# MLA attention: value products once per head and the causal mask accumulated by TensorE

## The reference, cut to what matters

```
s = (einsum('bqhd,bkhd->bhqk', qn_b, k_nope) + einsum('bqhd,bkd->bhqk', qr_b, k_rope)) * scale
s = where(kpos[None, :] <= qpos[:, None], s, -inf)
p = softmax(s, axis=-1)
o = einsum('bhqk,bkhd->bqhd', p, v)
```

## Time and profile before

| | |
|---|---|
| time, median of three runs | 3065.33 us (3062.18 to 3070.17) |
| the profiled execution's own time | 3056.96 us |
| its span in the trace | 3055.2 us |
| TensorE busy | 2800.9 us, 92% of the span |
| VectorE busy | 1583.5 us, 52% |
| ScalarE busy | 873.3 us, 29% |
| the attention block, from its first product to the end of its last copy | 2527.8 to 2611.1 us |

### The profile page before, as it was taken

One profiled execution on the slowest core, in us unless ns is written; L12 is line 12 of the kernel. 1 busy time (PEld: TensorE's weight loads), 2 busy tenths in 40 slices (PEclk: granted clock), 3 DMA queues, 4 the chain that ended last, 5 costly groups with the idle time before them and its releaser, 6 DMA issues. The chain is left out here.

```text
span 3055.2 us, 40875 instructions
## 1 busy us (share of the span) xinstructions
PE 2800.9 (92%) x17603; PEld 2207.4 (72%) x17603; DVE 1583.5 (52%) x2140; ACT 873.3 (29%) x1121; POOL 369.5 (12%) x352
## 2 busy tenths in 40 slices
PE   8999999687879899999999999799999669999997
PEld 6888876577755777788887854578887545688886
DVE  5555455666686834555545326463454545463342
ACT  3222234111134232322213423332222334432221
POOL 1111010212010001111100001121121000120110
PEclk9999999899989999999999988899999879999999
DMA  5555531000030033455553210223343200222331
GB/s 148 166 169 162 162 114 39 13 3 3 21 101 14 28 93 98 115 161 158 165 172 114 84 42 0 69 71 107 107 143 104 55 31 29 69 83 97 97 97 55
DMA packets 267301, 272.02 MB, mean 89 GB/s; under 512 B 12607, under 2 KB 248103, under 8 KB 266928
## 3 DMA queue, kind: packets, MB, share of 16 engines
q1 hardware_dynamic: 251760, 207.53, 22.2%
q0 software_dynamic: 15360, 61.87, 6.2%
HBM read 267.28 MB, written 2.10 MB: 88 GB/s over the span
## 5 line engine op out<-in xcount | busy, mean ns | idle before, releaser
L915 DVE TENSOR_TENSOR mix_wl<-ring_raw,mix_wh 128x2048 fp32r<-128x2048 f32 (+2 forms) x66 | 153.1, 2320 | 221.5 <-ACT mix_wh L807 221.5
L707 PE MATMUL mix_ps<-h_mix_hi,mix_wh 128*128 128x512 f32 x624 | 244.4, 392 | 0.0
L709 PE MATMUL mix_ps<-h_mix_lo,mix_wh 128*128 128x512 f32 x624 | 242.8, 389 | 0.0
L807 ACT ACTIVATE mix_wh<-ring_raw 128x2048 fp32r<-128x2048 f32 (+2 forms) x66 | 117.6, 1782 | 210.9 <-PE mix_ps L713 162.1
L707 PE MATMUL ffn_ps<-h_rw_hi,ffn_wh 128*128 128x512 f32 x448 | 175.3, 391 | 0.0
L709 PE MATMUL ffn_ps<-h_rw_lo,ffn_wh 128*128 128x512 f32 x448 | 174.3, 389 | 0.0
L915 DVE TENSOR_TENSOR mlp_wl<-ring_raw,mlp_wh 128x2048 fp32r<-128x2048 f32 (+1 forms) x38 | 96.7, 2545 | 131.1 <-ACT mlp_wh L807 131.1
L915 DVE TENSOR_TENSOR mlp_wl<-mlp_raw,mlp_wh 128x2048 fp32r<-128x2048 f32 x36 | 93.2, 2589 | 134.4 <-ACT mlp_wh L807 134.4
L713 PE MATMUL mix_ps<-h_mix_hi,mix_wl 128*128 128x512 f32 x624 | 154.2, 389 | 0.0
L707 PE MATMUL mlp_ps<-view,mlp_wh 128*128 128x512 f32 x384 | 150.1, 391 | 0.0
L709 PE MATMUL mlp_ps<-view,mlp_wh 128*128 128x512 f32 x384 | 149.5, 389 | 0.0
(11 more groups left out here) (577 smaller groups left out, 6202.1 us busy)
## 6 DMA issues: line engine op xcount, KB each, us to landing
ring_raw<-in_mlp_w SPq DMA_DIRECT2D x32, 1024.0 KB, 5.4
mlp_raw<-in_mlp_w SPq DMA_DIRECT2D x32, 1024.0 KB, 5.3
ffn_sraw<-in_ada_w POOLq DMA_DIRECT2D x34, 768.0 KB, 5.2
ffn_raw<-in_ffn_w_gu SPq DMA_DIRECT2D x44, 512.0 KB, 5.1
ring_raw<-in_ffn_w_gu SPq DMA_DIRECT2D x44, 512.0 KB, 5.0
mix_sraw<-in_ada_w POOLq DMA_DIRECT2D x22, 768.0 KB, 5.2
ring_raw<-in_w_in SPq DMA_DIRECT2D x14, 1024.0 KB, 5.4
ring_raw<-in_a_w_in SPq DMA_DIRECT2D x12, 1024.0 KB, 5.3
```

The source lines that it names most:

```text
L707: nc.tensor.matmul(ps[:, it.banks[t], :], w(h, k, t), xh[:, k, :], start=it.first and k == it.k0, stop=False)
L709: nc.tensor.matmul(ps[:, it.banks[t], :], w(h, k, t), xl[:, k, :], start=False, stop=False)
L807: nc.scalar.activation(slot(wh, it), slot(raw, it), ACT.Copy).then_inc(hi_ready, 1)
L915: nc.vector.tensor_tensor(slot(wl, it), slot(raw, it), slot(wh, it).bitcast(F32), ALU.subtract)\
```

## The change

In `mla_attention`:

- The mask is no longer added by VectorE. `scores` gets a third product, the identity matrix times the mask, 128 columns, added onto the diagonal block of the score tile by TensorE. It is this product that signals that the scores are ready.
- TensorE, and no longer VectorE, waits for the mask to be loaded, ahead of its first product.
- `values` is called once per head, in the step in which it was called for the head's last unit before. It multiplies the values of key block j with all the probabilities of the queries from j*128 on: four products of 512, 384, 256 and 128 columns in place of ten of 128.
- `pT` holds a whole head (four blocks of 512 columns), with two buffers (h % 2). `copies` writes its block row into it with a stride; it waits for the values of head h - 2 at a head's first unit, and not for those of three units ago at each unit.

```diff
-        p, pT = sb("p", [P, 3, L]), sb("pT", [P, 3, L])
+        p, pT = sb("p", [P, 3, L]), sb("pT", [P, 2, TT, L])
...
-                nc.tensor.matmul(pS[:, n % 3, 0:w], qr[0:ROPE, h, ts], kr[0:ROPE, 0:w], start=False, stop=True)\
+                nc.tensor.matmul(pS[:, n % 3, 0:w], qr[0:ROPE, h, ts], kr[0:ROPE, 0:w], start=False, stop=False)
+                nc.tensor.matmul(pS[:, n % 3, i * P:w], e.ident[:, :], mask[:, :], start=False, stop=True)\
                     .then_inc(s_done, 1)
...
-            def values(n):
-                h, i = units[n]
-                pe.wait_ge(pT_ready, n + 1)
-                if i == 0 and h >= 2:
+            def values(h):
+                pe.wait_ge(pT_ready, TT * (h + 1))
+                if h >= 2:
                     pe.wait_ge(out_done, h - 1)
-                for j in range(i + 1):
-                    last = nc.tensor.matmul(po[:, h % 2, i * P:(i + 1) * P], v[:, j, h * P:(h + 1) * P],
-                                            pT[:, n % 3, j * P:(j + 1) * P], start=j == 0, stop=j == i)
+                for j in range(TT):
+                    last = nc.tensor.matmul(po[:, h % 2, j * P:L], v[:, j, h * P:(h + 1) * P],
+                                            pT[:, h % 2, j, j * P:L], start=j == 0, stop=j == TT - 1)
                 last.then_inc(used, 1)
 
+            pe.wait_ge(loaded, 16)
             for n in range(N + 3):
...
-                if n >= 3:
-                    values(n - 3)
+                if n >= 3 and units[n - 3][1] == TT - 1:
+                    values(units[n - 3][0])
...
-                diag = pS[:, b, i * P:(i + 1) * P]
-                then(nc.vector.tensor_tensor(diag, diag, mask[:, :], ALU.add))
                 then(nc.vector.reduce_max(mx[:, b:b + 1], pS[:, b, 0:(i + 1) * P], AX.X))
...
-            dve.wait_ge(loaded, 16)
...
-                if n >= 3:
-                    act.wait_ge(used, n - 2)
-                nc.scalar.activation(pT[:, n % 3, 0:(i + 1) * P], pt[:, n % 3, 0:(i + 1) * P], ACT.Copy)\
+                if h >= 2 and i == 0:
+                    act.wait_ge(used, h - 1)
+                nc.scalar.activation(pT[:, h % 2, 0:i + 1, i * P:(i + 1) * P],
+                                     pt[:, n % 3, 0:(i + 1) * P].rearrange("p (j t) -> p j t", t=P), ACT.Copy)\
                     .then_inc(pT_ready, 1)
...
-                    act.wait_ge(used, n + 1)
+                    act.wait_ge(used, h + 1)
```

## The result

The changed kernel takes 3076.18 us (median of 7 runs, 3075.0 to 3081.76) against 3066.24 for the kernel before (7 runs, 3060.94 to 3070.26). The ratio is 1.0039, with a 95% interval of 1.0027 to 1.005: 10 us slower where 6.0 were predicted. The median lies 4.9 us above the 3071.3 of the forecast, inside the range of 3063 to 3079, but beyond the 0.3% within which the likeliest case lay.

What follows compares the result with a forecast made beforehand. The block was taken to be bound by what TensorE must issue, plus 0.60 + 0.2 us of waiting per head. Seven terms summed to +6.0 us, giving 3071.3 us on the median, range 3063 to 3079.

Steps and rivals of the forecast that it cites:

- mask products: 32 mask products added to TensorE's stream, 0.22 us each: +7.0 us, bounds +3.2 and +10.2.
- value products: Per head, 20 value instructions of 128 columns become 8 of 512 to 128: -0.7 us, bounds -1.2 and +1.0.
- wait for the copy, and the slow restart: TensorE's wait for ScalarE's copy and the slower values behind it go, 0.28 us in seven heads: -2.0 us.
- wait for VectorE: TensorE's 0.60 us wait per head shrinks to 0.27 without VectorE's mask add: -2.3 us, bounds 0 and -4.2.
- wait for the mask at the start: TensorE's first product in the block now waits for the mask's load: +1.8 us, bounds 1.5 and 2.3.
- clock at the start: The 2.7 us pause before TensorE's first product may lower its clock: +0.9 us, bounds 0 and 1.7.
- tail: After the last scores, values wait for the head's last copy, mostly at low clock: +1.3 us, bounds -0.4 and +2.1.
- rival (a): Between rope pair and turn, the mask pair costs 0.32 us: sum +9.2, or +10.0 with the high tail; chance 0.18.
- rival (b2): Loads of short value products are on the path; 96 fewer save 3.1 us, not 0.7: sum +3.6 us; chance 0.05.
- rival (c): The chain through VectorE bounds the block; each unit gains 0.33 us: sum -7.5 us; chance 0.04.
- Rival (b): The mask on TensorE is nearly free, 0.10 us a pair: sum +2.2 us; chance 0.07.
- (d): Long value products stream no faster per column: 1.7 us more, 3073.0 us; counted within the forecast's chance of 0.66.

Runs made afterwards that it cites:

- e13: The changed kernel profiled once more, unchanged; not timed, block 96.2 us against 93.2 in its first execution, cycle 10.46 us.
- e4: The changed kernel with four 256-column products, result unused, on TensorE during its wait for the mask; ratio 1.0013 to the kernel before, block 89.9 us.
- e5: The changed kernel with the mask product between the nope and rope products; ratio 1.0045 to the kernel before, cycle 10.17 us.
- e11: Like e9, but with the mask accumulated by TensorE as in the change; ratio 0.9997 to the kernel before, cycle 10.02 us.
- e3: The changed kernel with the mask loaded once in the program's first block and kept in SBUF; ratio 1.0020 to the kernel before, block 89.2 us.
- e1: The changed kernel with the mask added by VectorE again, so only the values once per head; ratio 1.0017 to the kernel before, cycle 9.90 us.
- e8: The kernel before, with VectorE normalising a head's third unit before the fourth unit's maximum; ratio 1.0005 to the kernel before, cycle 9.98 us.
- e9: e1 with VectorE's order of e8 and the last head's values per unit; ratio 0.9980 to the kernel before, block 76.8 us.
- e12: The kernel of e1 profiled once more, unchanged; not timed, cycle 9.90 us, block 89.4 us.
- e7: The changed kernel with the mask kept from the first block and multiplied in the one-pass float32 form; ratio 1.0020 to the kernel before, cycle 10.03 us.

## Why the prediction was right or wrong

The direction and the place held, and four of the seven terms within 0.2 us, a fifth within 0.4. Two did not, and together they are nearly the whole miss in the profiled executions. By the sign set down beforehand (wrong above a cycle of 10.4 us) the measured 10.46 says so too: the price of the mask pair was wrong. Term by term, in us over the whole block:

| step | predicted | measured in the changed kernel |
|---|---|---|
| mask products | +7.0 | 8 x 1.12 = +9.0 |
| value products | -0.7 | 8 x (2.15 - 2.24) = -0.7 |
| wait for the copy, and the slow restart | -2.0 | gone, -2.0 |
| wait for VectorE | -2.3 | 7 x -0.27 = -1.9 |
| wait for the mask at the start | +1.8 | 1.74 - 0.04 = +1.7 |
| clock at the start | +0.9 | +3.2 (e13: +6.1) |
| tail | +1.3 | 7.83 - 6.74 = +1.1 |
| sum | +6.0 | +10.4 of 10.5 |

The 1.12 us a head are 0.33 for the fourth unit less the 0.07 that its two transposes no longer pay, twice 0.32 less 0.05, and 0.32 for the first unit, where the transposes wait. The 2.24 us of the old values are 0.90, 0.67 and 0.22 from the rows, and 0.45 for the four behind the wait, whose delay is counted in the third line. In one cycle the same terms give 1.12 - 0.09 - 0.28 - 0.27 = 0.48, and measured are 10.46 - 9.97 = 0.49.

**The clock at the start was mis-sized.** I had the right event, a pause of 2.7 us in front of the first product, and gave it one spell of the length seen in the tail of the kernel before, 3.4 us, with half its cost for doubt. Both steps failed. The fall came in four of four executions with the pause, and the spells were 6.8, 6.8, 13.6 and 13.7 us long. The upper bound of 1.7 us was wrong because the length of a single spell, in another part of the kernel, was taken for the longest one. e4 shows the term by itself: with products in the pause it is gone.

**The mask pair was priced by the wrong row.** I chose the value pair at 0.22 us and argued that the change of rows behind the rope pair was paid already. That argument fails: the mask pair took 0.32, the price of my rival (a), and the transposes behind it gave back only 0.05 where they didn't wait. e5 shows that 0.22 is right for the place between the nope and the rope pair. The sentence of the prediction that failed is "the mask adds no such change". Rival (a), to which I gave 0.18, had the right price. That its sum with the high tail, +10.0, lies so near the measured +10.5 is luck: it gave nothing back, 1.2 us too much, and its clock term was 2.3 us too small.

**What held.** Eight value instructions take 2.15 us, predicted 2.16. Per instruction taken away the trace gives 0.09 / 12 = 7.5 ns; the starts are given to 0.01 us, so that the last digit is rough. The Trainium skill's figure, in "TensorE: Matmul & The Clock Gate", section Back-to-back issue gap, 25 ns between the two spacings (about 81 and 56 ns), would have given 0.30 us a head, an estimate from the page. The trace doesn't agree, and rival (b2) is out with it. The wait for the copies went, the wait for VectorE shrank from 0.66 (the transposes' start less the 0.42 us of the rope pair in front) to 0.39, and rival (c), the chain through VectorE as the bound, is refuted: the changed kernel takes the add out of that chain and its cycle grows by 0.49 us, and in e11 the four mask pairs lengthen a head by 0.71 us. Rival (b), a nearly free mask, is out by the same numbers, and (d) by the 2.15 us. The tail came out at +1.1 in this execution, but that is partly luck: in e3, whose tail does the same work, the clock was low there for 6.8 us and the end took 1.0 us more.

**What was missing.** The values once per head are worth nothing in this order of work (e1) and 6 us in another (e8 has none of them, e9 all). I had priced the edit by the stream around it and not asked which wait it would let go of next. The prediction also said that work taken from VectorE pays within the 0.60 us wait; e8 takes that whole wait away in the kernel before, and nothing is gained, because the wait for ScalarE's copy stands right behind it.

Slower by over 0.3% had a chance of 0.20 and happened. One result doesn't show that the chance was too low, but the reasoning does: the two errors, 2.3 and 2.0 us, have the same sign, and both stood in my text as open questions whose low or middle value I took. The range held the result because it was wide enough for rival (a), not because the terms were right.

## What to carry to other kernels

An add on an engine that has time to spare costs only what the bound engine waits for it; here that wait shrank by 0.27 us a head. The same add as a product on the engine that bounds the stage costs its price every time, here 0.28 us on average, four times a head. Before a buffer or a grouping is changed for its own sake, look for the wait that it will free: here the coarse values paid only after VectorE's order was changed, and the order only with the coarse values. And a wait put in front of TensorE's first instruction is to be counted with its clock: here filling it with products (e4) saved 3.2 us, and loading the operand in the program's first block (e3) saved 5.0 at the start.

## What the runs showed of the hardware

- A pause of 2.65 to 2.80 us in TensorE's stream was followed in four of four executions by 6.8 to 13.7 us at 1.2 GHz, beginning 1.8 to 1.9 us after the products had begun again. Eight instructions of 256 columns in that pause kept the clock at 2.4 GHz at the start (e4, one execution).
- The clock also fell inside a steady stream (e1, e12): cycles of 9.90 us with a wait of 0.82 us each ran at 1.00 for several heads, and then one didn't. The kernel before, with waits of 0.60 and 0.2 us in each cycle, had no such fall in the one execution profiled, nor had e8, with 0.69. The kind of products alone doesn't do it: nine other executions with the values once per head, and waits of at most 0.46 us in a cycle, had none in the middle of the block. Whether the length of the wait decides isn't shown, since no run changed it alone.
- After a fall the clock can stay low though products run without a gap: 13.6 us in e13, where the same kernel had 6.8 us in its first execution.
- A float32 product of 128 columns and 128 rows takes 0.32 us between a 64-row product and the transposes, which give back 0.05 of it (changed kernel), and adds 0.22 us between a 128-row and a 64-row one (e5); in the one-pass form it takes 0.17 us in the first of these places (e7).
